# Constant products on TensorE in the waits of a decoder layer's routing tail

## The reference

```
z = x @ w_in                                   # q | k | v | B | C | h
x = LayerNorm(alpha*x + concat(attention, B*conv3(C*h)) @ w_o)
g_prob = softmax(x @ w_rg + b_rg);  grp = argmax(g_prob)          # 1 of 4 groups
top_p, top_i = top_k(softmax(expert logits of that group), 2)     # 2 of its 8 experts
gate = g_prob[grp] * top_p / sum(top_p)
y = sum over the two experts of gate * (silu(x @ w_gate[e]) * (x @ w_up[e])) @ w_down[e]
x = LayerNorm(alpha*x + y)
```

## Time and profile before

| what | value |
|---|---|
| median of 3 runs | 2325.32 us (2319.47 to 2326.38) |
| profiled execution | 2324.31 us |
| its span, first to last instruction | 2322.2 us |
| mean granted clock of PE | 0.957 |
| PE busy | 2138.6 us, 92% |
| DVE, ACT, POOL busy | 30%, 14%, 14% |
| mean DMA traffic | 227 GB/s |

### The profile page before, as it was taken

How to read it: one execution, slowest core, us unless ns; L and a number is a source line. 1 busy time by engine, 2 the same in 40 slices (tenths; PEclk the granted TensorE clock), 3 DMA queues, 4 the chain that set the end, 5 groups by cost and what they waited for, 6 DMA issues and landing times.

```text
span 2322.2 us, 29399 instructions
## 1 busy us (share of the span) xinstructions
PE 2138.6 (92%) x9748; PEld 1406.5 (61%) x9748; DVE 699.0 (30%) x1343; ACT 335.0 (14%) x829; POOL 333.8 (14%) x440
## 2 busy tenths in 40 slices
PE   7899999969999999999589999999699999999993
PEld 5566655546666666666356666555566666666662
DVE  3602256661111111111364112766411111111116
ACT  2010123301111111111011011332011111111111
POOL 0200011111111111111232000211012111121113
PEclk8999999979999999999789999999799999999995
DMA  7511012345999999999461110213479999999964
GB/s 242 139 37 37 18 38 95 143 185 204 350 371 379 378 375 376 370 369 357 140 192 37 37 36 10 96 64 136 178 300 368 379 375 375 383 369 372 371 233 151
DMA packets 101660, 526.29 MB, mean 227 GB/s; under 512 B 16346, under 2 KB 25434, under 8 KB 84850
## 3 DMA queue, kind: packets, MB, share of 16 engines
q1 hardware_dynamic: 86738, 491.52, 55.0%
q0 software_dynamic: 14848, 33.85, 5.8%
HBM read 489.88 MB, written 58.27 MB: 236 GB/s over the span
## 4 chain that ended last, share of the span: by engine, by line
PE 83%; DVE 6%; issue 4%; DMA 3%; SPq 2%; ACT 1%; POOL 1%; DVEq 0%; POOLq 0%; ACTq 0%
PE ps L830 22%; PE ps L548 20%; PE ps L863 11%; PE ps L834 8%; PE ps L691 8%; PE ps L867 4%; PE ps L813 3%; PE ps L735 1%; DVE arena L1634 1%; DVE arena L1524 1%; DMA arena<-in_w_in 1%; DVE stat L1627 1%; PE ps L638 1%; PE ps L662 1%; PE ps L650 1%
## 5 line engine op out<-in xcount | busy, mean ns | idle before, releaser
L548 PE MATMUL ps<-arena 128*128 128x344 f32 x1728 | 510.3, 457 | 11.4 <-DMA arena<-in_w_in 8.0
L830 PE MATMUL ps<-arena 128*128 128x256 f32 x2304 | 511.6, 383 | 2.5 <-DVE arena L1524 2.5
L830 PEld LDWEIGHTS ps<-arena 128*128 128x128 f32 x2304 | 439.0, 192 | 88.2 <-issue 28.9
L548 PEld LDWEIGHTS ps<-arena 128*128 128x128 f32 x1728 | 329.4, 192 | 185.7 <-issue 20.4
L863 PE MATMUL ps<-arena 128*128 128x512 f32 x576 | 255.8, 597 | 20.3 <-ACT arena L1081 19.1
L1535 DVE SCALAR_TENSOR_TENSOR arena<-ps,gates,arena 128x256 f32<-128x256 f32 (+1 forms) x128 | 61.5, 480 | 665.9 <-ACT arena L1076 665.9
L1753 POOL DMA_INDIRECT ytok<-arena,scol x64 | 98.7, 1542 | 974.3 <-DVE arena L1548 618.4
L691 PE MATMUL ps<-arena 128*128 128x512 f32 x448 | 199.7, 604 | 3.1 <-ACT arena L1029 2.4
L834 PE MATMUL ps<-arena 128*64 128x256 f32 x896 | 199.4, 381 | 0.0
L836 PE MATMUL ps<-arena 128*64 128x256 f32 x896 | 199.4, 381 | 0.0
L863 PEld LDWEIGHTS ps<-arena 128*128 128x128 f32 x576 | 106.5, 190 | 148.3 <-issue 122.1
(11 more groups left out here) (231 smaller groups left out, 1720.4 us busy)
## 6 DMA issues: line engine op xcount, KB each, us to landing
arena<-in_w_gate SPq DMA_DIRECT2D x64, 2048.0 KB
arena<-in_w_up SPq DMA_DIRECT2D x64, 2048.0 KB, 20.2
arena<-in_w_down SPq DMA_DIRECT2D x64, 2048.0 KB, 20.3
arena<-in_w_in SPq DMA_DIRECT2D x36, 512.0 KB, 3.2
arena<-out_y_all SPq DMA_DIRECT2D x16, 512.0 KB, 3.2
xs<-arena SPq DMA_DIRECT2D x16, 512.0 KB, 2.6
ytok<-arena SPq DMA_DIRECT2D x16, 512.0 KB, 3.5
arena<-ytok SPq DMA_DIRECT2D x16, 512.0 KB, 7.3
```

Of the source, the lines that this page charges most:

```text
L548: last = mm(ps[:, 3 * half + ch, 0:CH], wring[:, slot, k * P:(k + 1) * P], xT[:, k, ch * CH:(ch + 1) * CH], start=(k == 0), stop=(k == KD ...
L830: last = mm(ps[:, 2 + q, at_c:at_c + 256], xgT[:, slot, k], w[slot][:, k, cols], start=(k == 0), stop=(k == KD - 1))
```

## The change

A helper multiplies the identity by the first of the attention masks, both constants that stay in SBUF, into the first 256 columns of bank 5, and it is called at four places of the tail: 5 products before `x1_transposed(8)`, 2 before `route(8)`, 11 before the last `ranks_within`, and 10 before the wait for `rk_done`. Nothing else changes.

```diff
+                def keep_busy(n):
+                    for _ in range(n):
+                        mm(ps[:, 5, 0:256], ident[:], masks[:, 0, :], start=True, stop=True)
+
                 early, late = slice(0, EARLY), slice(EARLY, NT)
                 out_project(8, mixT[:, 1], P, ((11, lambda: ranks_within(0, 0, early)),))
                 route(7, P, NB)
                 placed(0, early)
+                keep_busy(5)
                 x1_transposed(8, 0, P)
+                keep_busy(2)
                 route(8, P, NB)
+                keep_busy(11)
                 ranks_within(1, 2, late)
...
                 mm(ps[:, 2, 256:320], foundT, perm, start=True, stop=True).then_inc(s["rk_ranked"], 1)
+                keep_busy(10)
                 pe.wait_ge(s["rk_done"], BASE + l + 1)
```

## The result

The changed kernel takes 2313.0 us (median of 6 runs, 2309.5 to 2314.53) against 2325.35 us before (6 runs, 2319.47 to 2326.38). The ratio is 0.9949, 95% interval 0.9936 to 0.9962: 0.5% faster, and inside the forecast's range (2313, from 2309 to 2316). Run again later it was 2313.17 us, ratio 0.9961 [0.9947, 0.9975].

A forecast was written before the change was run, and what follows sets the result against it. TensorE, busy 92% of the span, bounds most of it, with half-clock stretches in each layer's tail. Gains of 5.80 and 5.63 us, together 11.4, take 2324.31 to 2312.9, stated as 2313; main case 2309 to 2316, full range 2308 to 2319.

The forecast's parts named there:

- X1 transposes and routing: Last tile of each layer at full clock: transposes gain 0.45 and 0.71 us, routing 1.73 in each layer.
- the second fill: Two products before routing: 0.86 us against 0.83 idle, so 0 to 0.1 late; 0.1 taken per layer.
- The gather's transposes with the copies behind them: Before the first expert: transposes take 1.09 us at full clock, not 1.95, gaining 0.86 per layer on the path.
- The 64 matmuls: First expert: 13.81 us at full clock against 16.97 and 16.54, gaining 3.16 and 2.73 on the path.
- The 0.3 for a late last fill: Before the first gather's transposes: ten products, begun at half clock, end 0 to 0.6 us late; 0.3 taken per layer.
- It moves by what routing moves: First gather lands behind expert 1's weights, 19.57 us after routing (19.89 in the second layer), and shifts with routing.
- The late placing: After the ranks: PE ends 1.0 us earlier, priced at nothing because the gather waits behind expert 1's weights.
- The third fill: Eleven products before the last ranks: 4.75 us against 5.29 idle, so covered with 0.5 to spare.
- The second: Rival: clock drops again between last fill and first expert; 1.75 us a layer, 2316.4, up to 2318.8; chance 0.18.
- The fourth: Rival: constant products don't raise or hold the clock, so fills run at half speed; 2338.7 us; chance 0.08.
- the third, that the gather lands when it did: Rival: gains before the gather, 2.1 and 2.3 us, are lost; 2317.3, up to 2323; chance 0.14.
- the rule on transposes: Trainium skill: transposes don't engage the full clock; first expert would start at half speed, 2318.8; the prediction rejected it.

The follow-up runs named there:

- no_last: Changed kernel without the last fill of 10 products; the fills of 5, 2 and 11 stay: 2317.87 us, ratio 0.9984 to the kernel before.
- last_only: Changed kernel with only the last fill of 10 products; the fills of 5, 2 and 11 are removed: 2318.39 us, ratio 0.9985 to the kernel before.
- no_eleven: Changed kernel without the fill of 11 products before the last ranks: 2312.29 us, ratio 0.9955 to the kernel before.
- last_five: Changed kernel with 5 products in place of 10 in the last fill: 2317.01 us, ratio 0.9970 to the kernel before.
- double: Changed kernel with every fill twice as long (10, 4, 22 and 20 products): 2335.14 us, ratio 1.0055 to the kernel before.
- turned: Changed kernel with all fills made of identity transposes (16, 6, 35 and 32) in place of products: 2312.15 us, ratio 0.9956 to the kernel before.
- held: `tuned` with three more products: one more behind the late placing, two in the wait for the turned table: 2308.30 us, ratio 0.9933 to the kernel before.
- tuned: Changed kernel with expert 1's weights behind the first gather, `rk_done` wait behind the gather's transposes, fills rearranged and added: 2309.69 us, ratio 0.9936 to the kernel before.
- after_again: The changed kernel itself, unaltered, measured again: 2313.17 us, ratio 0.9961 to the kernel before.

## Why the prediction was right

**The mechanism** is as told: the change takes no wait away; it moves the slow stretch from routing and the first expert onto products that nobody needs. `no_last` and `last_only` show its two halves separately. The forecast tail gain of 11.4 us was 10.98. That the median came out at 2313.0 to a tenth is luck: I had subtracted from an execution of 2324.31, the median before was 2325.35, and the ratio's interval means a gain of 9 to 15 us.

**The terms.** X1 transposes and routing, with the second fill between them: from 5.97 us (504.55 - 498.58) to 3.87, so 2.10 against 2.08 forecast; in the second layer 6.23 (1645.14 - 1638.91) to 3.88, so 2.35 against 2.34. The wait before routing stayed at 0.83, so the second fill cost nothing there; but routing took 1.95 us and not 1.87. The gather's transposes with the copies behind them: 0.81 and 0.82 against 0.86. The 64 matmuls: 2.89 and 2.46, forecast 3.16 and 2.73. Here the size was off by 0.27: I took 13.81 for the full clock, and the first expert takes 14.08 in the timeline. Most of that is a mix of two views: 13.81 is the second expert's in the chain, which counts from the end of the matmuls before it, and the timeline has the same 64 at 13.98. I should have set timeline beside timeline. The 0.3 for a late last fill didn't come in the first layer, where it ended 0.6 us ahead of the transposes; it took 6.41 us (6.95 in the second), within the 6.0 to 7.3 that the prediction's bounds mean. (It puts L801's end at 515.3; by its own terms that is 517.60 - 2.08 = 515.5, which changes nothing here.) In the second it ended where they start, and cost nothing measurable.

**The gather's landing.** "It moves by what routing moves" was off by 0.40 us in the first layer (19.57 to 19.97) and right to 0.05 in the second (19.89 to 19.94). The cause of the 0.40 is open. In the 16 tails of the eight kernels with this order of the weights and with fills no longer than these, the transposes start 19.3 to 20.3 us after routing. The order of SyncE's issues doesn't explain it: the down part of expert 1's weights was issued 3.23 us behind routing's end in the changed kernel's first layer, but in `no_last` it was 2.12 with 19.32 for the transposes, and in `last_only`'s second layer 1.79 with 20.29.

**The late placing.** Its price of nothing was right, and the reason was wrong. I had said that PE would end 1.0 us earlier and that the gather could be issued 1.0 earlier. In the first layer PE did place in 1.10 us in place of 1.97, but it then waited 0.82 for VectorE (L801 in the timeline, L794 before), a wait that did not show before. L801 starts 10.41 us after routing, as L794 did, and the gather is issued 13.29 us after it:

```profile
516.87 1.28 POOL L1743 DMA_INDIRECT arena<-xs,gcol  x1 [1.07 <-issue]
```

before 13.32 (517.87 - 504.55). So the DMA engines had nothing to take back: the gather was issued earlier by what routing gave, and by no more.

**The third fill** was covered, with 0.45 us to spare (0.5 forecast); the prediction didn't say that it was useless, and `no_eleven` shows it.

**The rivals.** The second, a drop between the last fill and the expert, is real, though not in the changed kernel's profiles: it came in `last_only` and in both layers of `last_five`. The fourth was wrong, as constants raise the clock; `double` shows what fills cost that are longer than their waits. Of the third, that the gather lands when it did, nothing came: the 0.40 us lie within what the profiles differ by. Of the rule on transposes, `turned` shows that it doesn't hold here. My own evidence against it, the start of the kernel, was weaker than I made it. Before, the clock was up behind the first 16 transposes, as the next eight show:

```profile
12.71 1.07 PE L519 MATMUL ps<-ident,arena 128*128 128x128 f32 x8 [2.08 <-DMA arena<-in_x_all]
```

In the changed kernel the same 16 were followed by eight in 1.94 us, the half clock (at 12.67). Its windows still show 1.00 there, as all of them do from 0 us on, when PE hasn't done anything: at the start of a profile the durations have to be read, not the clock's column.

## What to carry to other kernels

Look in the windows for stretches in which PE's granted clock is at its half, and count only the groups on the chain inside and just behind them: that, not PE's idle time, is what filling can buy. A fill must end before the work behind it is ready, as PE takes it in order, yet reach close enough to it that the pause doesn't undo it (2.25 and 2.63 us of waiting did in `last_five`, 1.09 did in `last_only`, 1.06 and 1.22 didn't in `held` and `turned`); read its length at both clocks and expect the slower. When a wait is shortened, ask which other wait stands at the same place: here VectorE's `rk_done` stood right behind the gather.

## What the runs showed of the hardware that was not expected

- The clock fell to its half (0.55 in 513 to 516 in `tuned`) behind a stretch in which PE was busy 2.43 of 3 us, mostly with products of 64 columns or fewer, and at the start of a wait of 1.18 us. With three more products of 256 columns (`held`) it stayed. They added work and at the same time shortened the waits there, from 0.34 to nothing and from 1.18 to 0.28 us; which of the two kept the clock isn't shown.
- The clock stayed up and rose over transposes of 32-bit floats alone as it did over products (`turned`: 1.00 in 500 to 509, and 14.08 us for the 64 matmuls behind 32 transposes).
- Profiles of identical source have the clock fall at other points of the layers (in the changed kernel's first profile around 336, 475 and 1473 us, of which `after_again` has only the first; before, around 475 and 1615). Against each other they show what such a drop costs, 1.4 to 1.6 us. That may be a good part of the spread of 5 to 10 us between runs of one kernel, but only one run of each has a profile. The changed kernel's tails agree to 0.3 us between two profiles (40.32 and 40.29, 40.04 and 40.26), so edits of 2 us are read better from the tails than from the medians.
